# Gate and up projections of a SwiGLU block in a seven-product (Winograd) form: 20 of 22 weight pairs, with all weight sums on VectorE

## What is computed

```python
  y = sum_b sigmoid(gate_b) * (branch_b @ w_br_b);  x = x + y @ w_out;  x = x + SwiGLU(RMSNorm(x))
Final RMSNorm.
```

## Time and profile before

| | us |
|---|---|
| runs shown | 990.56, 993.94, 994.91; median 993.94 |
| the profiled execution, its own time | 996.81 |
| its span, first to last instruction | 995.0 |
| PE busy | 967.9 (97%) |
| DVE busy | 507.7 (51%) |
| ACT busy | 335.9 (34%) |
| mean granted PE clock | 0.993 |

### The profile page before, as it was taken

How to read it: one execution, slowest core, us unless ns; L and a number is a source line. 1 busy time by engine, 2 the same in 40 slices (tenths; PEclk the granted TensorE clock), 3 DMA queues, 4 the chain that set the end, 5 groups by cost and what they waited for, 6 DMA issues and landing times.

```text
span 995.0 us, 18231 instructions
## 1 busy us (share of the span) xinstructions
PE 967.9 (97%) x7611; PEld 945.0 (95%) x7611; DVE 507.7 (51%) x933; ACT 335.9 (34%) x559; POOL 77.6 (8%) x107
## 2 busy tenths in 40 slices
PE   6999999999999899999999999999999999999997
PEld 5899999999989889899999999999999999999997
DVE  5735556544887472635355565554445555333232
ACT  7344223444544350422222342222222222222222
POOL 0100013011210200111023000000000000000000
PEclk9899999999999999999999999999999999999999
DMA  7582326432320766122222345222222222222302
GB/s 240 153 262 42 48 77 95 156 108 77 98 65 1 218 192 200 43 86 85 86 86 85 127 147 189 85 88 92 99 96 95 86 85 75 85 75 80 111 1 91
DMA packets 104909, 104.77 MB, mean 105 GB/s; under 512 B 11130, under 2 KB 101752, under 8 KB 104492
## 3 DMA queue, kind: packets, MB, share of 16 engines
q1 hardware_dynamic: 101224, 92.51, 30.3%
q0 software_dynamic: 3552, 11.08, 3.7%
q10 hardware_dynamic: 52, 0.01, 0.0%
HBM read 97.74 MB, written 15.45 MB: 114 GB/s over the span
## 4 chain that ended last, share of the span: by engine, by line
PE 86%; SPq 3%; DVE 3%; ACT 2%; issue 2%; DMA 1%; POOL 1%; ACTq 0%; DVEq 0%; POOLq 0%
PE acc L466 74%; SPq L698 3%; PE acc L1168 1%; PE acc L1081 1%; POOL mt L854 1%; PE acc L1057 1%; PE acc L935 1%; PE acc L924 1%; PE acc L895 1%; PE acc L1041 1%; PE acc L1252 1%; ACT h_hi L1562 1%; DVE w_lo L449 0%; PE acc L1069 0%; DVE mt L1670 0%
## 5 line engine op out<-in xcount | busy, mean ns | idle before, releaser
L466 PE MATMUL acc<-h_hi,w_hi 128*128 128x256 f32 (+1 forms) x1520 | 462.0, 304 | 3.1 <-DVE w_lo L449 2.1
L466 PE MATMUL acc<-h_lo,w_hi 128*128 128x256 f32 (+1 forms) x1520 | 439.2, 289 | 0.0
L466 PE MATMUL acc<-h_hi,w_lo 128*128 128x256 f32 (+1 forms) x1504 | 433.0, 288 | 0.0
L466 PEld LDWEIGHTS acc<-h_hi,w_hi 128*128 128x128 f32 x1520 | 287.6, 189 | 12.0 <-issue 5.1
L466 PEld LDWEIGHTS acc<-h_lo,w_hi 128*128 128x128 f32 x1520 | 288.0, 189 | 4.1 <-issue 2.4
L439 ACT ACTIVATE w_hi<-raw 128x1024 fp32r<-128x1024 f32 (+1 forms) x135 | 140.9, 1043 | 444.9 <-PE acc L466 444.9
L466 PEld LDWEIGHTS acc<-h_hi,w_lo 128*128 128x128 f32 x1504 | 285.0, 189 | 0.0
L449 DVE TENSOR_TENSOR w_lo<-raw,w_hi 128x1024 fp32r<-128x1024 f32 (+1 forms) x134 | 164.0, 1224 | 107.6 <-ACT w_hi L439 102.9
L466 PE MATMUL acc<-s_hi,w_hi 128*128 128x256 f32 (+1 forms) x352 | 101.6, 288 | 0.0
L466 PE MATMUL acc<-s_lo,w_hi 128*128 128x256 f32 (+1 forms) x352 | 101.3, 288 | 0.0
L466 PE MATMUL acc<-s_hi,w_lo 128*128 128x256 f32 (+1 forms) x352 | 100.7, 286 | 0.0
(11 more groups left out here) (348 smaller groups left out, 1122.6 us busy)
## 6 DMA issues: line engine op xcount, KB each, us to landing
raw<-in_w_in SPq DMA_DIRECT2D x25, 1024.0 KB, 5.3
raw<-in_w_gate_up SPq DMA_DIRECT2D x22, 1024.0 KB, 4.9
raw<-in_w_down SPq DMA_DIRECT2D x8, 1024.0 KB, 4.7
rev<-tab POOLq DMA_DIRECT2D x1, 4352.0 KB, 19.4
ring<-in_cache_dsa_kv SPq DMA_DIRECT2D x4, 1024.0 KB, 7.3
raw<-in_w_out SPq DMA_DIRECT2D x4, 1024.0 KB, 5.1
out<-in_cache_dsa_kv SPq DMA_DIRECT2D x2, 2016.0 KB
ring<-in_cache_moba_k SPq DMA_DIRECT2D x48, 64.0 KB, 2.1
```

Source lines behind the costliest of these rows:

```text
L466: ins = nc.tensor.matmul(acc[:, bank, 0:HALF[half]], a[:, k, :], two(b[:, kx + k, :], half), start=first and k == k0 and c == 0, stop=last ...
```

## The change

It works on pairs: a load of 256 columns is one pair (two blocks of 128 columns, m = 0 and 1), its 8 row slices are two groups (h = 0 and 1), the tokens two halves of TH = 272. A pair is then a 2 x 2 by 2 x 2 block product, with depth d = 4 slices (3 for the last chunk of down). In the plain form that is 8 products of d x 3 matmuls with 272 columns. In the seven-product form it is 7, of sums of weights and sums of activations. Of the 22 gate and up pairs the first and the last stay at eight (`EIGHT`), 20 are in `seven`. Down is done in three chunks (4, 4 and 3 pairs of up), each right after the first gate pair of the next chunk, all in eight products.

For one seven-pair the list of PE has the products 1, 6, 5, 7, 2 (1, 5, 6, 2, 7 where nothing is held), and 4 and 3 come after product 1 of the next pair (`held`). Each product is an item of `stream`, and `tm(i)` is the due time of item i. The sums are formed as follows. Weights: w5, w6, w7, w3 are four sums of 128 x 512, each one DVE instruction (`w_sums`). All seven operands are split, by ACT (`w_highs`) and DVE (`w_lows`), each 128 x 512, into six slots (`RING`); an operand is made when the item that last used its slot is done (`made_at`). Activations: `h_parts`, once, for all eight slots. Results: ACT (`bank_seeds`) copies the bank of product 1 to a second bank ("b"), after product 6 this bank to a third ("c") and to `u2p5`, and after 5 that bank to `u2p5`; DVE has four evacuations of 272 columns a pair (`results`), one instruction `second_half` of 544, and as before two for gating or for `s_lo`; ACT has two sigmoids (gate) or two `s_hi` (up), both in `gating`.

The core of the diff:

```diff
+        KPS = (4, 4, 3)
+        FIRST = (0, 4, 8)
+        EIGHT = (0, 21)
...
+        for c in range(len(KPS)):
+            for m_ in range(KPS[c]):
+                gate_or_up("gate", c, FIRST[c] + m_)
+                if m_ == 0 and c > 0:
+                    pairs += [("down", c - 1, j) for j in range(KD // 2)]
+                gate_or_up("up", c, FIRST[c] + m_)
+        pairs += [("down", len(KPS) - 1, j) for j in range(KD // 2)]
...
+            if n in seven:
+                stream += [(n, 1, 0, d)] + held + [(n, p, 0, d) for p in ((6, 5, 7, 2) if held else (5, 6, 2, 7))]
+                held = [(n, 4, 0, d), (n, 3, 0, d)]
...
+        RING, LEAD = 6, 5
...
+        def tm(i):
+            return n_wout + 0.25 * i
+        def made_at(u):
+            return tm(last_use[operands[u - RING]] + 1) if u >= RING else tm(u - LEAD) if u >= 4 else n_wout - 0.94 + 0.05 * u
...
+        term_order = sorted((made_at(op_at[n, q] if p in (7, 3) else min(op_at[n, 5], op_at[n, 6])) - 0.25 * early, n, p) for n in seven
+                            for p, q, early in ((5, 5, 2.2), (6, 6, 2), (7, 7, 1.6), (3, 3, 1.6)))
...
+        def lag(n, t):
+            return tm(last_item[n] + t)
+        T_SIG, T_GATE = 1.8, 3.6
...
+                def product(i):
...
+                    pe.wait_ge(w_lo_done, n_wout + u + 1)
+                    if n in seven:
+                        name = {1: "a", 2: "a", 5: "e", 3: "e", 6: "b", 7: "c", 4: "c"}[p]
+                        opens, closes = p in (1, 5), k1 == depth(n)
+                        if p in (6, 7):
+                            pe.wait_ge(seeded, seeds[n, "b" if p == 6 else "c"])
+                        if p == 4:
+                            pe.wait_ge(ffn_ev, evacs[n, "22"])
...
+                def bank_seeds():
+                    for i, n, what in copies:
+                        yield tm(i + 1)
+                        act.wait_ge(mm_done, products_done + i + 1)
...
+                        nc.scalar.copy(dst, src).then_inc(seeded, 1)
+                def gating():    
+                    for n, (kind, c, j) in enumerate(pairs):
+                        if kind == "gate":
+                            yield lag(n, T_SIG)
+                            if n in seven:
+                                act.wait_ge(ffn_n2, halves[n])
...
+                            for m in range(2):
+                                nc.scalar.activation(sg[:, m, :], ga[:, m, :], ACT.Sigmoid).then_inc(sem("sg_done"), 1)
+                        if kind == "up":
+                            for m in range(2):
+                                yield part_time(n, m)
+                                if n in seven:
+                                    act.wait_ge(ffn_n2, halves[n])
...
+                                b_his(4 + j, slice(2 * m, 2 * m + 2), s4_hi[:, j - FIRST[c]])
...
+                def w_sums():
+                    for time, n, p in term_order:
+                        yield time
+                        if p == 5:
+                            w_ready(dve, n)
+                            terms = w_sum(n, 0), w_part(n, 1, 0), w_part(n, 1, 1)
...
+                        nc.vector.tensor_tensor(*terms, ALU.add).then_inc(sem("w_sum"), 1)
+                def w_lows():
+                    for u, (n, p) in enumerate(operands):
+                        yield made_at(u) + 0.01
+                        dve.wait_ge(w_hi_done, n_wout + u + 1)
+                        nc.vector.tensor_tensor(w_slot(u, True), w_source(n, p), w_slot(u, False).bitcast(F32),
+                                                ALU.subtract).then_inc(w_lo_done, 1)
...
+                def second_half():
+                    for n in sorted(seven):
+                        kind = pairs[n][0]
+                        yield lag(n, 1.1)
+                        dve.wait_ge(ffn_ev, evacs[n, "12"])
+                        if kind == "gate":
+                            x = ga[:, :, 0:TH]
+                            nc.vector.tensor_tensor(x, x, rstd[:, 0:TH].unsqueeze(1).broadcast_to([P, 2, TH]), ALU.mult).then_inc(ffn_n2, 1)
...
-        DOWN = ((0, 8), (8, 16), (16, 22))
-                    if w == n_wout:
-                        return lambda half, k: pe.wait_ge(sem("h2_lo_done"), k + 1)
-                    if w >= n_gu:
-                        return lambda half, k: pe.wait_ge(sem("s_lo_done"), k + 1)
```

More of the change, by code:

```diff
@@ L187, in build @@
         xT = keep("xT", [P, KD, T])
+        h_at = keep.at
         h_hi = keep("h_hi", [P, KD, T], F32R)
@@ L355, in build @@
         n_wout = len(blocks)
[L356 to L359, removed]
-        DOWN = ((0, 8), (8, 16), (16, 22))
[L361 to L364, removed]
+        n_all = n_wout
+        ffn_load = len(loads)
@@ new lines, in build, with gate_or_up @@
+        KPS = (4, 4, 3)
+        FIRST = (0, 4, 8)
+        EIGHT = (0, 21)
+        pairs, seven = [], set()
+        def gate_or_up(kind, c, j):
+            if sum(p[0] != "down" for p in pairs) not in EIGHT:
+                seven.add(len(pairs))
+            pairs.append((kind, c, j))
+        for c in range(len(KPS)):
[4 more added lines that the diff above has]
+                gate_or_up("up", c, FIRST[c] + m_)
@@ new lines, in build, with depth @@
+        pairs += [("down", len(KPS) - 1, j) for j in range(KD // 2)]
+        NPAIR = len(pairs)
+        for kind, c, j in pairs:
+            if kind == "down":
+                k0 = 2 * FIRST[c]
+                loads.append(([(0, 0, rows(w_dn, k0, k0 + 2 * KPS[c], 2 * j * P, 256))], 2 * P))
+            else:
+                loads.append(([(0, 0, rows(w_gu, 0, KD, (D_FF if kind == "up" else 0) + 2 * j * P, 256))], 2 * P))
+        def depth(n):
+            return KPS[pairs[n][1]] if pairs[n][0] == "down" else KD // 2
@@ new lines, in build @@
+        results_at = []
+        for i, (n, p, k0, k1) in enumerate(stream):
+            if n in seven and p in DONE:
+                results_at.append((i, i + 1, n, DONE[p]))
+            elif n not in seven and p[1] == 1 and k1 == depth(n):
+                name = f"{p[0] + 1}{p[2]}"
+                results_at.append((i, i + (3.5 if pairs[n][0] != "down" and p[0] == 0 else 1), n, name))
+        assert [r[1] for r in results_at] == sorted(r[1] for r in results_at)
+        evacs = {(n, name): i + 1 for i, (_, _, n, name) in enumerate(results_at)}
@@ new lines, in build @@
+        evac_time = {(n, name): t for _, t, n, name in results_at}
+        copies = []
+        for i, (n, p, k0, k1) in enumerate(stream):
+            if n in seven and p in (1, 5, 6):
+                copies.append((i, n, {1: "b", 5: "p5", 6: "c"}[p]))
+                if p == (5 if pos[n, 6] < pos[n, 5] else 6):
+                    copies.append((i, n, "u2"))
+        seeds = {(n, what): i + 1 for i, (_, n, what) in enumerate(copies)}
+        halves = {n: i + 1 for i, n in enumerate(sorted(seven))}
@@ L1522, in feed @@
                 def feed():
-                    yield n_wout + 0.7
+                    yield tm(2.5)
                     act.wait_ge(sem("ssq_mm"), 1)
                     for half in range(2):
-                        nc.scalar.activation(two(rstd, half), acc[:, 6 + half, 0:HALF[half]], ACT.Sqrt, bias=eps[:, :],
+                        nc.scalar.activation(two(ssq, half), acc[:, OLD[4 + half], 0:HALF[half]], ACT.Sqrt, bias=eps[:, :],
                                              scale=1.0 / D).then_inc(sem("std_done"), 1)
[L1528 to L1539, removed]
```

469 lines of the change are left out of this document (368 added, 101 removed).

## The result

The changed kernel takes **1029.98 us** (median of 4), the kernel before 993.6 beside it: ratio 1.0376, 95% interval 1.0338 to 1.0415. That is slower, as forecast, but by 36 us and not by 8, and above the range. The profiled execution took 1029.33 us with a span of 1027.5; before it was 996.81 and 995.0.

The account below looks back on a forecast made before the run. PE's matmul count times pitch was taken to bound the kernel. Removed matmuls -30.1, new waits +35.9, start and end +2.5 gave +8.3 us: 1005.1 profiled, 1002 against the median; forecast range 997 to 1007, 8-in-10 range 984 to 1019.

Parts of the forecast that it names:

- What bounds the kernel before, and what is removed: Gate, up and down: time is matmul count times 125.5 ns pitch; 240 matmuls fewer give -30.1 us.
- Prices: Instruction times on DVE and ACT and handoffs, such as 0.61 us per 512 columns on DVE, 0.43 per 272-column copy.
- The five small matmuls: Start of the stage: five small matmuls more take 0.5 us.
- The wait that I expect: Ahead of product 7, PE waits 2.2 us per pair for copy c behind sigmoids; +35.9 us in all.
- The second part of the walk: Seven-pairs with PE late: product 4 may start at 4.7 us, period 12.9 in the mean, 2.33 over 10.54.
- Start and end: Stage start and kernel end: PE waits some 0.7 us for the sum of squares; all additions together +2.5 us.
- The lag of DVE: First 28 items: DVE has 38.5 of about 40 us of work; 0.8 us of lag taken (0 to 4).
- Rival 4: Seven-pair items: PE's clock falls, at 0.95 over 190 us costing 10 us more; 1009 us, chance 0.1.
- rival 1: Product 7: DVE has enough air, ACT's queue costs only its floor, 0.95 us late each; 982 us, chance 0.11.
- Rival 3: Seven-pairs: DVE instructions don't overlap, each 0.08 us longer, some 14.1 us a period; 1020 us, chance 0.1.
- Rival 2: Seven-pairs: the cover holds, copy c is never late; 965 us, chance 0.06.
- Rival 5: Seven-pairs: quicker handoffs, period is DVE's work plus idle time, 12.3 us; 993 us, chance 0.2.

Follow-up runs that it names:

- run 12: Changed kernel with ACT's and DVE's lists reordered, second pair's sums and splits later, and `over_rms` moved into the first four down pairs: 972.55 us.
- Run 1: Changed kernel with ACT's list alone reordered, sigmoids or `s_hi` behind copy c and w_hi 3 of the next pair: 1000.27 us.
- run 2: Changed kernel with DVE's list alone reordered, weight sums 3, 5 and 6 just behind `second_half`: 999.61 us.
- run 4: Changed kernel with the second norm due at item 6, its root at 6.5 and reciprocal at 7.1 (before 2, 2.5, 3.1): 1027.6 us.
- run 8: Changed kernel with 14 matmuls of 272 columns that nobody reads put ahead of PE's wait for copy c: 1017.49 us.
- Run 6: Kernel of run 5 with operand 3's split and the second pair's sums and splits later, `over_rms` back to back behind the reciprocal: 1012.59 us.
- run 11: Changed kernel with sigmoids behind copy c, sums 5 and 6 behind `second_half`, gating earlier, plus one unread 512-column DVE sum per seven-pair: 988.12 us.
- runs 3 to 6: The first of these: changed kernel with product 2 ahead of product 7 in PE's list, 1027.59 us; the others are run 4, run 5 and Run 6.
- run 5: Changed kernel with both reorderings, ACT's list as in Run 1 and DVE's list as in run 2: 1013.05 us.

## Why the prediction was right and wrong

- **What bounds the kernel before, and what is removed:** right. 2928 matmuls at 0.1256 us, down pairs without waits.
- **Prices:** right to a few hundredths: 512 columns start 0.60 us apart on DVE (0.61), a copy of 272 takes 0.37 (0.43), from `second_half` to product 7 it is 2.37 us (2.4). The five small matmuls were underpriced: 0.5 us forecast, some 1.2 at full clock (run 12).
- **The wait that I expect:** right in place, count and size. Run 1 took it away and run 2 brought it down to its floor, each by the order of one list. The second part of the walk (PE late, product 4 at 4.7 us, period 12.9, mean 2.33) was right as well at full clock: 12.74 and 13.11 us in run 4, 12.90 in the mean in run 8, and in every second period product 4 waits 0.3 us beside the 2.1 of product 7. In the ten periods with a half-rate stretch the 0.3 is gone; that slow matmuls give DVE the time for it is a likely reason, not tested.
- **Start and end:** here a term of the sum was mis-sized, "PE waits some 0.7". PE waited 4.6 us. I took the last sum of squares from the kernel before, and hadn't set the six new DVE instructions of 512 columns (3.6 us) ahead of the evacuation that it needs (L1973). DVE's timeline in the kernel after:

```profile
580.48 1.29 DVE L2054 TENSOR_TENSOR wx_lo<-raw,wx_hi 128x512 fp32r<-128x512 f32 x2
581.68 1.29 DVE L2054 TENSOR_TENSOR w_lo<-raw,w_hi 128x512 fp32r<-128x512 f32 x2
582.88 0.69 DVE L2047 TENSOR_TENSOR wsum<-raw 128x512 f32<-128x512 f32 x1
583.60 0.69 DVE L2047 TENSOR_TENSOR wsum<-wsum,raw 128x512 f32<-128x512 f32 x1
584.21 0.42 DVE L1973 TENSOR_TENSOR xT<-acc,xT 128x256 f32<-128x256 f32 x1
...
587.59 0.72 DVE L1982 TENSOR_TENSOR ssq<-ssq,sq 128x544 f32<-128x544 f32 x1 [1.36 <-ACT sq L1751]
```

  Run 6 brought the wait down to 2.1. The norm's matmuls then ran at the lower clock, 3.8 us in place of 2.05 (run 12, at full clock). The lag of DVE (0.8 forecast) showed as the wait of 2.8.
- **Rival 4, PE's clock falls:** this is the step that failed. I gave it a chance of 0.1, and 10 us, from a stretch where the clock was 0.77 with PE 87% busy, and left it out of the sum because another stretch at 85% had 1.00. It was worth 17.5 us of half-rate matmuls in the stage and 1.8 more in the norm's; run 8 gave back 12 us of it, with copy c as late as before. And I had treated it as another case beside my forecast, where it is a consequence of it: once the sum says that PE stands still for 2.2 us 14 times, the clock belongs in the same sum.
- **Rivals 1, 2, 3 and 5:** rival 1's floor (0.95) is what run 2 shows (0.87). Rival 3, DVE without overlap, is refuted: starts lie 0.60 us apart. Its own sum had a slip: 11.5 + 2.25 is 13.75 us a period and not 14.1, so some 1016 in place of 1020. DVE's throughput bound nothing in the changed kernel (window: 14.9 of 20 us); it does once the orders are mended and 0.6 us of work is added per pair (run 11). Rival 2 needed a copy c that is never late, which this order doesn't give. Rival 5 needed quicker handoffs, and the chain of 2.37 us shows them as priced.

**What stays open:** which waits take the clock down. In the pairs of the changed kernel and of runs 3 to 6, leaving out the waits of the start, 30 of the 49 waits of 2.1 us and more (up to 2.65) had a half-rate stretch behind them: 10 of 14, 3 of 7, 8 of 14, 5 of 7 and 4 of 7. None of the shorter ones (0.6 to 1.95 us) had, nor any of the 31 in runs 1 and 2. What decides among the 49 isn't shown, and no run varied the wait alone.

## What to carry to other kernels

When an engine becomes nearly full and works through a fixed list, write that list out for one period and follow the chain through both engines: the wait came from two instructions standing ahead of a copy, not from the amount of work, and moving due times alone turned 3.8% slower into 1.1% faster. If the sum then says that PE will stand still for some 2 us again and again, put a lower clock behind a good half of these into the same sum (here 30 of 49). Repairs interact through waits (run 5), so walk the combination too.

## What the runs showed of the hardware

- Behind 10 of 14 waits of PE of 2.1 us came 3.2 us at half rate (14 matmuls of 272 columns 0.23 us apart). The length was nearly the same each time; the beginning lay anywhere from 0 to 1.5 us after the end of the wait. Matmuls whose results nobody reads, put into the wait, kept the clock up and made the kernel 12 us faster.
- While GpSimd ran a `TENSOR_TENSOR` of 544 columns (1.7 us each), DVE's `TENSOR_TENSOR` of 512 columns took 1.85 us in place of 0.69, while its reciprocal of one input took 3.54 as always. The Trainium skill (SBUF — State Buffer, "Who interferes with whom") says that a `tensor_tensor` with both inputs in SBUF contends with GpSimd's reads, and that the shared port pair is an exclusive lock; the trace agrees: while both worked, DVE's started 1.76 us apart, about as long as one of GpSimd's takes.
